# The last three expert blocks added in PSUM by one-hot products, assignment rows loaded ahead of the convolution's weights

## The reference

```python
def second_block(...):
    h = concatenate([meta, x])
    for i in range(2):
        mixed = rglru_mixer(h, ...) if i == 0 else shortconv_mixer(h, ...)
        h = layer_norm(ALPHA * h + mixed, ln_g[i, 0], ln_b[i, 0])
        ffn = hierarchical_moe(h, ...)
        h = layer_norm(ALPHA * h + ffn, ln_g[i, 1], ln_b[i, 1])
    return h[:, 16:]

def hierarchical_moe(h, ...):
    # a group of 8 experts by argmax, the best 2 experts in it; gates = pg * softmax of the two
    ...
    y = zeros.at[slot_tok].add(ys * slot_gate[:, None])
```

## Time and profile before

| | us |
|---|---|
| median of 3 runs | 2272.41 |
| lowest and highest run | 2269.43, 2273.7 |
| span of the profiled execution | 2270.0 |
| TensorE busy | 2095.8 (92%) |
| TensorE weight loads busy | 1218.6 (54%) |
| VectorE busy | 801.5 (35%) |
| ScalarE busy | 535.4 (24%) |
| GpSimd busy | 254.3 (11%) |

### The profile page before, as it was taken

One profiled execution on the slowest core, in us unless ns is written; L12 is line 12 of the kernel. 1 busy time (PEld: TensorE's weight loads), 2 busy tenths in 40 slices (PEclk: granted clock), 3 DMA queues, 4 the chain that ended last, 5 costly groups with the idle time before them and its releaser, 6 DMA issues. The chain is left out here.

```text
span 2270.0 us, 28982 instructions
## 1 busy us (share of the span) xinstructions
PE 2095.8 (92%) x11658; PEld 1218.6 (54%) x11658; DVE 801.5 (35%) x1734; ACT 535.4 (24%) x1229; POOL 254.3 (11%) x266
## 2 busy tenths in 40 slices
PE   7999999999999999969999898959996999989995
PEld 3446643444445577445555454548864555545552
DVE  2055325442555489452111011157745211111113
ACT  1123221022664145112212111130001212112112
POOL 0000000210111311101111111101200111111102
PEclk9999998999999999969999999979997999999998
DMA  9415243042003111259999999981134999999995
GB/s 357 143 48 186 79 165 122 32 154 74 1 1 115 75 52 73 76 225 405 426 423 424 423 422 418 417 316 45 68 149 177 366 423 424 422 424 423 423 423 203
DMA packets 101226, 545.98 MB, mean 241 GB/s; under 512 B 13424, under 2 KB 27545, under 8 KB 67146
## 3 DMA queue, kind: packets, MB, share of 16 engines
q1 hardware_dynamic: 82016, 506.22, 55.2%
q0 software_dynamic: 18592, 37.46, 4.7%
q10 hardware_dynamic: 474, 0.33, 0.1%
HBM read 538.86 MB, written 28.94 MB: 250 GB/s over the span
## 5 line engine op out<-in xcount | busy, mean ns | idle before, releaser
L847 PE MATMUL ps<-arena,ring 128*128 128x512 f32 (+8 forms) x1440 | 424.0, 453 | 9.7 <-DVE arena L2535 2.2
L1406 PE MATMUL ps<-ring,arena 128*64 128x256 f32 x3296 | 375.3, 384 | 5.8 <-ACT arena L1915 3.2
L847 PEld LDWEIGHTS ps<-arena,ring 128*128 128x128 f32 x1440 | 258.0, 193 | 164.8 <-issue 136.3
L1406 PEld LDWEIGHTS ps<-ring,arena 128*64 128x64 f32 x3296 | 233.6, 138 | 127.6 <-DMA ring<-in_moe_w_up_dram 4.4
L938 PE MATMUL ps<-ring,arena 128*128 128x512 f32 x528 | 234.3, 600 | 3.0 <-DVE arena L2303 1.3
L2660 DVE SCALAR_TENSOR_TENSOR arena<-arena,ps 128x256 f32<-128x256 f32 x78 | 32.8, 421 | 565.3 <-ACT arena L1925 565.3
L1419 PE MATMUL ps<-ring,arena 128*64 128x512 f32 x880 | 207.8, 616 | 24.4 <-DMA ring<-in_moe_w_down_dram 24.4
L1406 PE MATMUL ps<-arena 128*64 128x256 f32 x1696 | 192.6, 381 | 0.0
L3027 POOL DMA_INDIRECT assignment_rows<-arena x78 | 82.4, 1057 | 794.4 <-ACT arena L1931 765.2
L938 PEld LDWEIGHTS ps<-ring,arena 128*128 128x128 f32 x528 | 99.6, 192 | 124.9 <-issue 123.0
L1406 PEld LDWEIGHTS ps<-arena 128*64 128x64 f32 x1696 | 119.4, 137 | 60.5
(11 more groups left out here) (370 smaller groups left out, 2084.0 us busy)
## 6 DMA issues: line engine op xcount, KB each, us to landing
ring<-in_moe_w_down_dram SPq DMA_DIRECT2D x45, 2048.0 KB, 27.9
ring<-in_moe_w_up_dram SPq DMA_DIRECT2D x44, 2048.0 KB, 26.5
ring<-in_moe_w_gate_dram SPq DMA_DIRECT2D x43, 2048.0 KB, 24.2
arena<-in_moe_w_gate_dram SPq DMA_DIRECT2D x21, 2048.0 KB, 26.1
arena<-in_moe_w_up_dram SPq DMA_DIRECT2D x20, 2048.0 KB, 26.1
arena<-in_moe_w_down_dram SPq DMA_DIRECT2D x19, 2048.0 KB, 29.1
ring<-in_ada_w_dram SPq DMA_DIRECT2D x12, 2048.0 KB, 12.0
ring<-in_a_w_in_dram SPq DMA_DIRECT2D x12, 1536.0 KB, 13.9
```

Source lines behind the costliest of these rows:

```text
L847: ins = pe.matmul(dst, w, m, start=i == 0, stop=i == len(pairs) - 1)
L1406: ins = pe.matmul(ps[CAP * i:CAP * (i + 1), bank_, 256 * j:256 * (j + 1)], rows_t[:, k, :], w[:, k, 256 * i:256 * (i + 1)], start=k == 0, ...
```

## The change

Late blocks. The last three blocks of each layer (`LATE`) are no longer scattered. Their rows stay in SBUF; for each tile of tokens TensorE adds them in PSUM by products with one-hot rows (slot by token), 64 rows at a time, on top of the tile itself, which it brings into PSUM by the identity in two products (`late_start`, `late_blocks`). The tile then stands in PSUM, and the statistics and ScalarE's rescaling read it there.

Other rows. `ya_d` is cleared early in the program by two DMAs of ScalarE, since rows of late blocks are never written to it. The assignment rows are loaded by SyncE right behind the last slabs of the stage, into two of the lent places and the norm's buffer; all weights of the convolution come after them. VectorE and GpSimd add them to the tiles without gates (`partial`), ahead of the late sums. Tile 2 of layer 1 is added by TensorE (`late_rest`).

Gates. A second set of one-hot products (`slot_gates`) gives the gate of every slot, and `yo_copy` scales by it.

Order. The overflow count is written ahead of the reading of the table, and TensorE tests it ahead of the blocks, with a copy of the blocks in both branches; ScalarE and VectorE test it ahead of the last block. GpSimd loads the last norm's vectors without a scatter before them. The tail's order of tiles is 0, 2, 3, 1 instead of 0 to 3.

```diff
+LATE = 3
+EARLY = NBS - LATE
# sync, experts(l)
-                if l == 0:
-                    for turn in range(first + 3 * NE, first + 3 * NE + 2):
-                        dense(turn)
-                sp.wait_ge(y_ready, NBS * (l + 1))
                 sp.wait_ge(route_ready, l + 1)
                 n_over = sp.value_load(over_i[0:1, NOVER:NOVER + 1], min_val=0, max_val=NOVER)
...
                 for par in range(2):
                     sp.wait_ge(yo_sent[par], SENT(l, par))
+                for turn in YIN_TURNS[l]:
+                    sp.wait_ge(*consumed(turn))
                 for t in ((4, 0, 1, 2, 3), range(NT))[l]:
                     r = rows_of(t)
-                    sp.dma_start(yin[t][0:r], ya_d[l][2 * P * t:2 * P * t + 2 * r, :].rearrange("(p k) d -> p k d", k=2))\
-                      .then_inc(yin_in[t], 16)
+                    sp.dma_start(yin(l, t)[0:r], ya_d[l][2 * P * t:2 * P * t + 2 * r, :].rearrange("(p k) d -> p k d", k=2))\
+                      .then_inc(tile_in[t], 16)
# tensor
+            def slot_gates(l):
+                n = 10 if l == 0 else 8
+                for i in range(n):
+                    r = rows_of(i // 2)
+                    pe.wait_ge(hot_ready, (0, 20)[l] + n + i + 1)
+                    ins = pe.matmul(ps[:, bank(f"table{l}") + 1, 0:NBLK], row_hot[0:r, i, :], block_hot[0:r, i, :], start=i == 0, stop=i == n - 1)
+                ins.then_inc(gates_made, 1)
...
+            def late_start(l, t):
...
+                for h in range(2):
+                    pe.matmul(ps[0:r, late_bank(l, t) + h, :], ident[0:r, 0:r], X[0:r, t, 512 * h:512 * h + 512], start=True, stop=False)
+            def late_blocks(l, t):
...
+                for i in range(LATE):
+                    B = NBS * l + EARLY + i
+                    pe.wait_ge(yo_ready, B + 1)
+                    hot = late_meta[i] if t == 4 else late_hot[i][:, P * t:P * (t + 1)]
+                    for h in range(2):
+                        s = slice(CAP * h, CAP * (h + 1))
+                        ins = pe.matmul(ps[0:r, late_bank(l, t) + h, :], hot[s, :], yo_of(B)[s, :], start=False, ...)
...
+            def experts(l):
                 pe.wait_ge(route_ready, l + 1)
                 n_over = pe.value_load(over_i[0:1, NOVER:NOVER + 1], min_val=0, max_val=NOVER)
                 with pe.If(n_over > 0):
+                    blocks(l)
+                    over_blocks(l, n_over)
                 with pe.Else():
+                    blocks(l)
...
+            late_sum(0, 4)
+            late_sum(0, 0)
+            late_sum(0, 1)
             turn_tile(4, 4)
+            late_sum(0, 2)
             turn_tile(4, 0)
             turn_tile(4, 1)
+            late_sum(0, 3)
             start_early(first, 4, 0, 0, META + P)
...
+            late_start(1, 2)
+            late_sum(1, 0)
+            late_blocks(1, 2)
+            late_rest(1, 2)
+            late_sum(1, 3)
+            late_sum(1, 1)
# scalar
+            for l in range(2):
+                z = a["zero_row"]
+                act.dma_start(ya_d[l], bass.AP(z.tensor, z.offset, [[0, 2 * (TM, S)[l]], [1, D]])).then_inc(zeros_in, 16)
...
-                act.activation(yo[B % 2], ps[:, 6 + B % 2, :], ACT.Copy).then_inc(yo_ready, 1)
+                act.activation(yo_of(B), ps[:, 6 + B % 2, :], ACT.Copy, scale=gate_of[:, n:n + 1]).then_inc(yo_ready, 1)
# vector, route(l): the five steps of ovt, ovf and over_i (2648 to 2652) now stand ahead of done(vec, "table"), and then
+                for i in range(2 * nt):
+                    vec.tensor_scalar(block_hot[:, i, :], block_no, place[:, 10 + i:11 + i], gates[:, i % 2, i // 2:i // 2 + 1],
+                                      ALU.is_equal, ALU.mult).then_inc(hot_ready, 1)
...
+                ins = vec.tensor_copy(gate_of, ps[:, bank(name) + 1, 0:NBLK])
+            def late_hots(l):
+                for i in range(LATE):
...
+                    vec.tensor_scalar(late_hot[i], late_hot[i], late_tok[:, i:i + 1], None, ALU.is_equal).then_inc(late_built, 1)
+            def partial(l, t):
...
+                step(vec.tensor_tensor(x, x, y[:, 0, :], ALU.add))
+                vec.tensor_tensor(x, x, y[:, 1, :], ALU.add).then_inc(partial_ready, 1)
# gpsimd, experts(l)
-                    scatter(l, n)
+                    if n < EARLY:
+                        scatter(l, n)
+                    if n == EARLY - 1:
+                        late_columns(l)
```

## The result

The changed kernel takes 2289.9 us (median of 4 runs, 2286.95 to 2295.74) against 2273.05 of the kernel before (4 runs, 2269.43 to 2275.33). The ratio is 1.0078, 95% interval 1.0058 to 1.0098: slower by 13 to 22 us. The forecast was 6.2 us slower, 2278.6, with a range up to 2290.0. The direction was right, the size was not.

What follows compares the result with a forecast made beforehand. Expert stages were taken as bound by DMA rate, seam and tail by waits for memory. Routing 4.4, seam -0.9 and tail 2.7 summed to 6.2 us slower, median 2278.6; range 2269.5 to 2290.

Steps and rivals of the forecast that it cites:

- Something comes back: Start of both expert stages: TensorE, just busy with gates, runs first blocks at the higher clock, regaining 1.3 and 2.8 us.
- the heads: Start of both expert stages: branch and gates' products delay first transposes 5.1 and 3.4 us; net cost 4.4 us.
- the seam: Behind the first expert stage: TensorE's sums of five tiles replace waiting for memory; a gain of 0.9 us.
- the tail: Behind the last expert block: 22.0 us of sums replace scatter and load, 16.1 us follow; 2.7 us later.
- with no clock: Bound for the start of both expert stages, with no time regained by a higher clock: 8.5 us cost.
- Rival 1: Branch ahead of the blocks costs little, its target already fetched: whole change 3 us slower, 2275.5; chance 0.20.
- the norm's load: Last norm's vectors load ahead of layer 1's last slab: 2.5 us more, less 0.6 for the scatter.
- 2: Rival at seam and tail: all six products overlap, a tile's sum costs half; 14 us gained, 2264.6; chance 0.12.
- 4: Rival at seam and tail: pairs of 64-row products don't overlap; 24 us more, 2302; chance 0.04.
- Rival 3: TensorE waits long enough in seam or tail for its clock to fall: 10 us more, 2288; chance 0.13.
- rival 5: Early zero fill blocks ScalarE, so attention's exponentials wait: 12 us, 2290; chance 0.05.
- Layer 0's stage: From first transposes to the end of the last block in layer 0: forecast 1.9 us shorter.

Runs made afterwards that it cites:

- the head undone: Changed kernel with TensorE's overflow test ahead of block 33 and VectorE's five overflow steps behind the token numbers: 2282.2 us, ratio 1.0038 against the kernel before.

## Why the prediction was right in its direction and wrong in its size

**The step that failed is "Something comes back".** The prediction took 1.3 and 2.8 us off, because TensorE would have worked on the gates right before the first block. The first blocks took 8.55 and 9.56 us, against 8.44 and 9.93 before: in sum 0.3 came back instead of 4.1, and 0.3 is far within what first blocks differ by in the fourteen traces, 8.44 to 10.12. The trace of before had the answer: its clock was at 0.50 while the table's products ran, which are of the same form and count, and still at 0.52 in the slice 1014.20 to 1017.00. I had taken "busy" for what raises the clock; with the head undone, 40 such records within 10.7 us left it at 0.50.

Of the 10.5 us by which the stretches miss the forecast (16.65 against 6.15), this step is 3.8, the largest single one. The heads are 2.05, the seam 2.3 (within its spread), the rest of the two stages 2.25, the tail nothing. The prediction had the case "with no clock" as a bound, 8.5 us for the heads; the heads alone came to 10.55.

**The head itself was under-sized**, 5.1 and 3.4 against 5.82 and 4.73: the branch took 4.20 and 5.05, not 3.72. The prediction read its two records of 3.72 as one beside a busy DMA and one beside an idle one; during them the queues moved 147 and 97 GB/s, so neither told about a full queue, where the branch later took 5.94 to 6.50 us. The Trainium skill, "Runtime: NRT & Kernel Launch", section "Instruction fetch mechanics", says that a taken branch out of the fetched pages waits for a fetch. The wait did recur at the head, as the prediction had it by that rule; that it is one for a fetch, no run here shows. Rival 1, the cheap branch, is out. Undoing this head gave back 10.2 us at the heads themselves, less 2.2 behind them in layer 0: 8 of the 16.9.

**The seam's mechanism was right, its sum was not shown to be.** A tile of 4.69 was taken as 4.6, and the two waits of 1.7 and 1.5 as 1.98 and 2.08; those are small. The forecast of a gain of 0.9, 0.6 of it ahead of the last product, had no room for the turns' own waits (2.13 us ahead of the third one, by "issue"). In this trace it came out as a loss of 1.2, with 0.85 more up to the next routing. Both are within what traces with the same seam differ by, in part through the clock. Taking GpSimd out of it turned it into a gain: 260.11 against 262.71 before, and 36.8 us instead of 39.8 from the last product to the group of 80 records.

**The tail was right**: 21.8 us of sums (22.0), 16.3 behind them (16.1), and the norm's load ahead of the last slab, 2.63 net if the first block's 0.37 is set apart (1.9), whose price alone was 3.2 (2.5). What the prediction did not ask is why 16 us were needed; 6.4 of them were an order.

**Of the rivals**, 2 is out with tiles at 4.69, and 4 with it: 64-row products did run two at a time (twelve records in 2.85 us). Rival 3, the clock, did not come in seam or tail of the changed kernel's trace (1.00 from 1493.8 to 1521.0 and from 2250.0 to the last sum), but it did in the seam of four other runs, for about 1.5 us each time and not 10 in all. The zero fill of rival 5 delayed nothing that shows: the slot table begins at 997.0 to 1005.3 with it, at 1000.07 without. That it costs nothing was not tried by moving it. Layer 0's stage, 1.03 longer where 1.9 of gain had been forecast, is 2.9 off; 1.4 of that is the clock (8.55 for 7.13), the rest is open.

One reading of the slices was too wide: 417 to 426 GB/s holds inside the two expert stages, and the slices at their edges have 203 to 405. Nothing in the sum hangs on it.

## What to carry to other kernels

A test that stood where an engine waits anyway is free, and the same test ahead of the work is not: before moving one, look for a place where enough is queued to cover it, as behind block 16 in layer 0. A busy engine is not a fast one: read the granted clock of the very rows that are to be extended. And where a change swaps waits for work, its gain depends on who makes the inputs of that work: here a test, a load, two engines that shared the adds, and an order on a third hid a gain of 0.5%, which came out when these four were changed and one late block was given up.

## What the runs showed of the hardware that was not expected

The same kind of branch takes 3.7 to 6.5 us on TensorE and under 0.1 us on the other engines: ScalarE's test ahead of the last block took 0.045 to 0.054, GpSimd's 0.050, VectorE's 0.062 to 0.072. On TensorE it took 4.20 and 5.05 us with all 39 blocks standing twice, 5.94 to 6.50 with 23 or six of them, and 3.72 ahead of the overflow code alone, so a longer copy does not make it longer.

What goes along with it is the traffic. Over the 28 branches in the fourteen traces it took 3.72 us while the DMA queues moved 97 and 147 GB/s, 4.20 to 4.22 at 190 to 196, 4.85 to 5.05 at 286 to 297, and 5.94 to 6.50 at 410 to 435. Place and traffic changed together in these runs, so which of them sets the time stays open.

TensorE's granted clock did not go by its waits alone: at the seam of one run it fell to 0.50 behind waits of 2.07 and 2.13 us, in another it stayed at 1.00 behind 1.98, 2.08 and 2.13.
